# A streaming encoder step on one Trainium2 core: rows of the first norm rounded by ScalarE, scores ahead of the table turns, ten pairs between retrievals, first gates asked for among the up products

## The reference

```
h = rmsnorm(x) ; cb,cc,ch,q,k,v,rg,ga,gb = split(h @ w_in)            # 9 x 1024 columns
conv = causal width-3 convolution of cc*ch, times cb
ret  = chunked retention of rope(q), rope(k), v, 4 heads of 256, with decays and a carried state,
       group norm, times silu(rg)
x += (sigmoid(ga)*conv + sigmoid(gb)*ret) @ w_out
h = rmsnorm(x) ; per token and each of 8 heads: the top 16 of 128x128 product keys
x += sum over picks of softmax(score) * gelu(u[e] . h) * v[e]          # 16384 experts, rows of 1024
y = rmsnorm(x)
```

## Time and profile before

| | |
|---|---|
| median of 3 runs | 2223.83 us (2220.51 to 2227.95) |
| the profiled execution, its own time | 2224.73 us |
| its span, first to last instruction | 2222.9 us (1.8 us of the time lie around it) |
| mean granted TensorE clock | 0.994 |
| PE busy | 2166.9 us, 97% of the span |
| DVE busy | 1730.2 us, 78% |
| POOL busy | 866.3 us, 39% |
| ACT busy | 592.8 us, 27% |
| mean DMA rate | 331 GB/s |

### The profile page before, as it was taken

The page is one execution under the profiler, slowest core; times in us unless marked ns, Lnnn a source line. Parts: engine busy times, 40 slices in busy tenths (PEclk is TensorE's granted clock), DMA queues, the critical chain, the costliest instruction groups (busy, mean ns, idle before and its releaser), DMA issues.

```text
span 2222.9 us, 30818 instructions
## 1 busy us (share of the span) xinstructions
PE 2166.9 (97%) x10473; PEld 1692.8 (76%) x10473; DVE 1730.2 (78%) x3244; ACT 592.8 (27%) x1159; POOL 866.3 (39%) x606
## 2 busy tenths in 40 slices
PE   5999999999999999999999999999999999999998
PEld 5989889899998885655565565577767777777776
DVE  3566675667675285988988989999949898888987
ACT  3212222122223111121221211233324333333333
POOL 4322122223333004576675684512114454454540
PEclk9999999999999999999999999999999999999999
DMA  4999899999983367999999999888899999999993
GB/s 161 304 306 320 288 303 307 318 321 312 309 286 143 108 219 304 355 370 412 403 402 412 389 411 413 337 274 289 292 320 393 413 414 414 413 414 414 414 412 141
DMA packets 314151, 735.40 MB, mean 331 GB/s; under 512 B 30368, under 2 KB 163232, under 8 KB 314016
## 3 DMA queue, kind: packets, MB, share of 16 engines
q1 hardware_dynamic: 189792, 439.67, 54.8%
q0 software_dynamic: 73728, 268.47, 30.6%
q10 hardware_dynamic: 50496, 25.59, 3.8%
HBM read 604.04 MB, written 129.57 MB: 330 GB/s over the span
## 4 chain that ended last, share of the span: by engine, by line
PE 61%; DVE 16%; DMA 7%; issue 6%; POOL 6%; SPq 2%; ACT 1%; DVEq 0%; ACTq 0%; POOLq 0%
PE ps L1750 7%; PE ps L1808 7%; PE ps L1807 7%; PE ps L1809 7%; PE ps L1710 6%; POOL b L679 5%; PE ps L1515 5%; PE ps L1514 5%; DMA b<-in_u_t 5%; PE ps L1516 5%; PE ps L1815 4%; PE ps L1765 3%; DVE b L1392 3%; DMA b<-in_peer_v,b 2%; DVE b L1032 1%
## 5 line engine op out<-in xcount | busy, mean ns | idle before, releaser
L1750 PE MATMUL ps<-b,b 128*128 128x384 f32 x2048 | 665.6, 486 | 0.0
L679 POOL DMA_INDIRECT b<-u_rows,b x256 | 367.2, 1434 | 717.3 <-DVE b L1375 517.9
L1750 PEld LDWEIGHTS ps<-b,b 128*128 128x128 f32 x2048 | 386.8, 190 | 263.4
L644 POOL TENSOR_TENSOR b<-b,b 128x1024 fp32r<-128x1024 f32 x80 | 195.1, 2442 | 468.9 <-ACT b L692 464.4
L1514 PE MATMUL ps<-b,b 128*128 128x320 f32 x1152 | 365.0, 317 | 1.6 <-issue 1.6
L1516 PE MATMUL ps<-b,b 128*128 128x320 f32 x1152 | 357.6, 310 | 0.0
L1515 PE MATMUL ps<-b,b 128*128 128x320 f32 x1152 | 357.5, 310 | 0.0
L1392 DVE SCALAR_TENSOR_TENSOR b<-b,b,b 128x1024 f32<-128x1024 f32 x256 | 330.9, 1292 | 28.3 <-DMA b<-in_peer_v,b 11.2
L1375 DVE CUSTOM_DVE_ANT_0 b<-b,b 128x1024 f32<-128x1024 f32 x256 | 312.5, 1221 | 28.4 <-DMA b<-u_rows,b 22.2
L679 POOL DMA_INDIRECT b<-in_peer_v,b x256 | 291.0, 1137 | 88.6 <-issue 78.3
L1032 DVE STREAM_TRANSPOSE b<-b 128x1024 f32<-128x1024 f32 x128 | 156.9, 1238 | 169.3 <-DMA b<-in_u_t 162.7
(11 more groups left out here) (164 smaller groups left out, 2588.0 us busy)
## 6 DMA issues: line engine op xcount, KB each, us to landing
b<-in_u_t SPq DMA_DIRECT2D x256, 512.0 KB, 5.5
u_rows<-b SPq DMA_DIRECT2D x512, 128.0 KB, 4.3
b<-in_peer_v SPq DMA_DIRECT2D x128, 512.0 KB
b<-in_w_in SPq DMA_DIRECT2D x72, 512.0 KB
b<-in_wq SPq DMA_DIRECT2D x48, 512.0 KB
acts<-b SPq DMA_DIRECT2D x128, 192.0 KB
gates<-b ACTq DMA_DIRECT2D x12, 2048.0 KB
b<-gates SPq DMA_DIRECT2D x32, 768.0 KB
```

Source lines behind the costliest of these rows:

```text
L644: nc.gpsimd.tensor_tensor(lo[u][:, :], raw[:, u, :], hi[u][:, :].bitcast(F32), ALU.subtract).then_inc(lo_ready, 1)
L679: nc.gpsimd.indirect_dma_start(slots[n % SLOTS][:, :], None, u_rows if kind == "u" else v_rows, bass.IndirectOffsetOnAxis(ap=row_id[:, r_ ...
L1750: last = nc.tensor.matmul(ps[:, e % 4, 0:TD], w[:, k * P:(k + 1) * P], h2[:, k, SD:T], start=(k == 0), stop=(k == KT - 1))
```

## The change

It does six things. ACT, not DVE, rounds the rows of the first norm (`rows_high`), and DVE squares and sums the last two of the five tiles. PE's transposes of that norm go to banks 2 to 7 in rotation (`norm_bank`), so that the first product, in banks 0 and 1, no longer waits for the roundings; POOL's `low(A, 0, 0)` moves ahead of all row tiles. In DVE's `scores` the turns stand behind the five multiplications. GAP goes from 11 to 10 and BEFORE_DOWNS from 1 to 6, so three pairs less come before the one-hots and two less among the down products (80 pairs are done when `weigh(0)` is reached, 78 before); all indices for picks, scores and gates move forward by one to three up products. SP reads the first group's activations and gates back within the up products 124 and 126, and the second group behind the first down tile.

```diff
-BEFORE_DOWNS = 1
+BEFORE_DOWNS = 6
+ACTS_AT = 124
+GATES_AT = 126
+SUMS_BY_ACT = 3
-EXP_AT = {1: 7, 2: 36, 3: 64, 4: 93}
-SCORES_AT = {2: 6, 3: 45, 4: 73}
-PICKT_AT = {2: 41, 3: 69, 4: 98}
-GATE_AT = 99
+EXP_AT = {1: 7, 2: 35, 3: 62, 4: 90}
+SCORES_AT = {2: 6, 3: 44, 4: 71}
+PICKT_AT = {2: 40, 3: 67, 4: 95}
+GATE_AT = 96
-GAP = 11
+GAP = 10
-    e = RETRIEVAL_AT + 28.6 * turn + (0.5 + 2.0 * i if i < INSIDE else 17.3 + 0.97 * (i - INSIDE))
+    e = RETRIEVAL_AT + 27.6 * turn + (0.5 + 2.0 * i if i < INSIDE else 17.3 + 0.97 * (i - INSIDE))
...
+def norm_bank(which, tt, b):
+
+    return b if which else 2 + 2 * (tt % 3) + b
...
+            def acts_in(g):
+                for i in range(2):
+                    sp.wait_ge(a_stored[i], 16 * (GROUP // 2) * (g + 1))
+                src = acts[g, :, :, :].rearrange("p k t -> p (k t)")
+                sp.dma_start(al[:, g % 2, :, :].rearrange("p k t -> p (k t)"), src).then_inc(al_loaded[g % 2], 16)
+            def gates_in(g):
+                src = gates[g, :, :, :]
+                sp.dma_start(gr[:, g % 2, :, :, :].rearrange("p b k t -> p b (k t)"), src).then_inc(g_loaded[g % 2], 16)
+            def group_in(g):
+                if g >= 2:
+                    sp.wait_ge(p_ready, (g - 1) * GROUP)
+                gates_in(g)
+                acts_in(g)
...
                 plain_in(3 * A_WQ + e, io["u_t"][e, :, :])
                 if e >= GROUP:
                     acts_out(e - GROUP)
+                if e == ACTS_AT:
+                    sp.wait_ge(onehot_used, TD // 4)
+                    acts_in(0)
+                if e == GATES_AT:
                     for i in range(2):
                         sp.wait_ge(gt_stored[i], 16 * (NB // 2))
+                    gates_in(0)
...
                 down_in(u)
                 acts_out(NKEY - GROUP + u)
                 if u == 0:
-                    group_in(0)
-            group_in(1)
+                    group_in(1)
...
+            low(A, 0, 0)
             for tt in range(TT):
-                if tt == TT - 2:
-                    low(A, 0, 0)
                 rows_low(0, tt, hf)
             for u in range(1, GROUP):
...
-            for tt in range(TT):
+            for tt in range(SUMS_BY_ACT):
                 act.wait_ge(x_loaded[tt], 16)
-                if tt >= 3:
-                    act.wait_ge(sum_done, tt - 2)
-                bank = 2 + 2 * (tt % 3)
+                bank = 2 + 2 * tt
                 nc.scalar.activation(ps[:, bank:bank + 2, :].rearrange("p a b -> p (a b)"), x[:, tt, :], ACT.Square,
                                      accum_out=ss[:, tt:tt + 1]).then_inc(sum_done, 1)
             act.wait_ge(sum_done, TT)
             nc.scalar.activation(rms[:, :], ss[:, :], ACT.Sqrt, bias=eps[:, 0:1], scale=1.0 / D).then_inc(rms_ready, TT)
-            for tt in range(TT):
+            def rows_high(tt):
+                for b in range(2):
+                    act.wait_ge(f_ready, 2 * tt + b + 1)
+                    f = hf[:, b, :].rearrange("p (k t) -> p k t", k=4)
+                    nc.scalar.activation(h_hi[:, 4 * b:4 * b + 4, tt * P:(tt + 1) * P], f, ACT.Copy).then_inc(h_split, 1)
+
+            scale_rows(0, 0, xs)
+            high_a(0, 0, 0, False)
+            for tt in range(1, TT):
                 scale_rows(0, tt, xs)
-                if tt == 1:
-                    high_a(0, 0, 0, False)
+                rows_high(tt - 1)
+            rows_high(TT - 1)
             high_a(1, 1, 1, False)
...
                     f = hf_[:, b, :].rearrange("p (k t) -> p k t", k=4)
-                    hs = (slice(None), slice(4 * b, 4 * b + 4), slice(tt * P, (tt + 1) * P))
-                    line.then(nc.vector.tensor_tensor(f, src, gb, ALU.mult))
-                    nc.vector.tensor_copy(h_hi[hs], f).then_inc(h_split, 1)
-
+                    nc.vector.tensor_tensor(f, src, gb, ALU.mult).then_inc(f_ready, 1)
+
+            for tt in range(SUMS_BY_ACT, TT):
+                dve.wait_ge(x_loaded[tt], 16)
+                squares = yret[:, 2 * (tt - SUMS_BY_ACT):2 * (tt - SUMS_BY_ACT) + 2, :].rearrange("p a b -> p (a b)")
+                nc.vector.tensor_tensor_reduce(squares[:, 0:D], x[:, tt, :], x[:, tt, :], 1.0, 0.0, ALU.mult, ALU.add,
+                                               ss[:, tt:tt + 1]).then_inc(sum_done, 1)
             dve.wait_ge(consts, 16 * 2)
             row_factor(0, 0, TT)
...
             def scores(g, r):
 
                 dve.wait_ge(tabs_loaded, g * 48 + 48)
-                if isinstance(g, int) and g == 0:
-                    turn(16, 2)
                 for j in range(PT + 1):
                     if j == 3:
                         for s in range(PT):
                             then(nc.vector.tensor_scalar(kw[:, s, :], kv[:, s, 0:DK], key_decay(g, s), None, ALU.mult),
                                  kw_ready, g * 12 + (s + 1))
-                        turn(0, 2, r, PER_HEAD)
                     dve.wait_ge(att_done, g * 5 + (j + 1))
                     bank, n = [5, 6, 7, 4, 5][j], att_n[j]
                     then(nc.vector.tensor_tensor(att[:, att_at[j]:att_at[j] + n], ps[:, bank, 0:n],
                                                  dec[:, 0:n] if j < PT else dec_s[:, :], ALU.mult),
                          att_ready, g * 5 + (j + 1))
+                if isinstance(g, int) and g == 0:
+                    turn(16, 2)
                 for s in range(KW - PT):
                     stream_keys(g, s)
                 for i in range(2):
                     then(nc.vector.tensor_tensor(qg[i], qT[:, i, PROMPT:T], gq[:, :], ALU.mult),
                          qg_ready, g * 2 + (i + 1))
+                turn(0, 2, r, PER_HEAD)
...
                     tok = slice(hv * HALF, (hv + 1) * HALF)
                     if rows_from is not None:
 
-                        pe.wait_ge(h_split, rows_from + 2 * TT - 1 + hv)
                         pe.wait_ge(h_ready, rows_from + 2 * -(-(hv + 1) * HALF // P))
...
-                    if tt:
-                        pe.wait_ge(h_ready if which else h_split, which * 2 * TT + 2 * (tt - 1) + b + 1)
+                    if which and tt:
+                        pe.wait_ge(h_ready, which * 2 * TT + 2 * (tt - 1) + b + 1)
+                    if not which and tt >= 3:
+                        pe.wait_ge(f_ready, 2 * (tt - 3) + b + 1)
                     for k in range(4):
                         cols = slice((4 * b + k) * P, (4 * b + k + 1) * P)
-                        last = nc.tensor.transpose(ps[:, b, k * P:(k + 1) * P], xs_[:, tt % 2, cols], ident[:, :])
+                        last = nc.tensor.transpose(ps[:, norm_bank(which, tt, b), k * P:(k + 1) * P], xs_[:, tt % 2, cols],
+                                                   ident[:, :])
```

More of the change, by code:

```diff
@@ L378, in build_program @@
         xsT_done = sem("xsT_done")
+        f_ready = sem("normed_rows_turned")
         h_split = sem("h_split")
@@ L999, in split_rows @@
                     gb = gain[:, 4 * b:4 * b + 4].unsqueeze(2).broadcast_to([P, 4, P])
-                    src = ps[:, b, :].rearrange("p (k t) -> p k t", k=4)
+                    src = ps[:, norm_bank(which, tt, b), :].rearrange("p (k t) -> p k t", k=4)
                     if which == 1:
```

## The result

The changed kernel takes 2230.5 us in the median, the kernel before 2224.4; the ratio is 1.0024, 95% interval 1.0017 to 1.0032. That is slower by a quarter of a per cent, where 2204 was forecast. The profiled execution has a span of 2229.9 us against 2222.9.

The account below looks back on a forecast made before the run. TensorE, busy 2166.9 of 2222.9 us, was taken as the bound, so only its waits and the slow matmuls behind them could shrink. Start 3, mixer 12 and picks 4.5 gave 19.5 us: 2204 by the median, range 2194 to 2214.

Parts of the forecast that it names:

- Gates early, six pairs before the downs: End of the up products: six pairs and the early gates' read stay hidden behind them; 0, from -2 to +1 us.
- That chain is unchanged: Up-to-down transition: ScalarE's way out, its rounding, DVE's two subtractions, first down product stay as before; 0, from -2 to +1.
- The start: First norm: roundings moved to ScalarE bring the first product from 33.26 to 30.3; gain 3 us, from 0 to 5.
- The mixer: Scores ahead of turns, four rounds: old waits go, some for the prompt state's copy appear; gain 12 us, 4 to 21.5.
- rival A: Mixer: waits only move to the prompt state's copy in all four rounds, eating all but 3 us; 2213, chance 0.20.
- Ten pairs: Between retrievals: each pair left out saves DVE 6.5 us, so TensorE's waits for picks go; gain 4.5 us.
- rival C: Between retrievals: pairs cost DVE only its own time, 4.8 us each, so waits for picks grow; 2211, chance 0.10.
- The rival on the other side: Mixer: both moved turns wait their whole loads, prompt state comes 7.4 us later each round; slower, 2244, chance 0.04.

## Why the prediction was wrong

**Gates early, six pairs before the downs** is the step that failed: "Hidden; without that cover each us costs one", taken as 0, from -2 to +1. It cost 17.6 in the trace, 14.8 of it wait and most of the rest the slow matmuls behind it. Three things in it were wrong. First, the store has no price in the step at all. It took at most 13.8 us before, and 44 with more gathers beside it. Second, the cover was counted in TensorE's products, from 119 to 126, seven of 5.16 us. But 126 is a place in SP's list, and SP runs ahead of TensorE: it reached the read at 1631.6, as product 122 ended, 15.7 us after the store was issued. A store of 14 us would just have fitted. "SP may wait there a little" named the place; the wait was 28.3 us. Third, I looked only at DVE for the six pairs ("each needs ScalarE's gelu"), not at POOL and the transfers, though the row with a share of 1.03 was in front of me and used for another step. The section of the Trainium skill that the prediction cites (DMA: Bandwidth & Descriptors, Issuing engines are not separate DMA queues), one set of 16 engines for all, I applied to the pairs and not to the store beside them.

**That chain is unchanged** (from ScalarE's way out at 1667.20 to the first down product 3.3 us later): it held in the changed kernel, 1674.12 to 1677.43. It is only that everything came late in front of it.

**The start:** 3 was forecast, with the first product at 30.3; it began at 28.4, from 33.26, and the lead at the first round was 5.4. The mechanism was right. The half buffers went round in 2.8 us a tile, not 3.1, because the rounding of 512 columns took 0.63 and the handings over were short, and the first difference began at 18.95, not 19.4:

```profile
18.95 2.50 POOL L672 TENSOR_TENSOR b<-b,b 128x512 fp32r<-128x512 f32 x2
...
21.75 2.50 POOL L672 TENSOR_TENSOR b<-b,b 128x512 fp32r<-128x512 f32 x2 [0.30 <-ACT b L760]
...
24.55 2.51 POOL L672 TENSOR_TENSOR b<-b,b 128x512 fp32r<-128x512 f32 x2 [0.29 <-ACT b L760]
```

**The mixer:** 12 was forecast, 2.0 came in this trace, and the runs with and without the new order differ by less than they can tell. The old waits went, as forecast, and were replaced, which is rival A's way. Round 1's new wait and slow matmuls were 5.1 where 4 were forecast, round 4's 6.3 where 4.7 were. The term failed in rounds 2 and 3, forecast at under 1 and with "more room": 2.4 and 3.5. The copy did come earlier in round 2, ending at 235.6 and not at the forecast 238.8; but TensorE wanted it at some 233, and not at 238.0, for the start's gain had not been taken off its time. The terms were added as if each stood alone. And the copy hangs on DVE's own row from `rotate_q` on, 17.5 us without a wait for a tile in round 2; only the run that took the turns out of that row showed this.

**Ten pairs:** 4.5 was forecast and 4.8 came between the first query products and the last up product, where rival C had a loss of 2; in the other traces with ten pairs it is 2.6 to 5.0. What was not in the forecast is that the three pairs left out cost 4 to 5 us among the down products and 1 to 2 in the last norm if nothing takes them up ahead of them. Six ahead did that, at the price above; three do it too.

With these sizes the sum is 5.4 + 2.0 - 1.5 (the `in_wq` waits) + 4.8 - 17.6 = -6.9, which is how late the trace ends. They are stretches of one trace, so they have to add up.

**The rival on the other side** (D, turns without cover, 2244) was slower for another reason than the one that came: the new waits in the mixer never reached 7.3 a round. No rival had a transfer that takes longer because of what the change puts beside it.

Could the 44 us have been seen ahead? An upper estimate from the kernel before was within reach. The store itself holds the engines 7 us. Six pairs gather 24 times 128 rows of 4 KB, 12.6 MB, which is 31 us at the 412 GB/s of the earlier trace rows. If all of it goes first, the store needs 38 us, and more with the tiles, against a cover of 15.7. That it does nearly all go first only the later runs show. How much of the start's gain a given execution keeps varies by a few us between traces of one order, and why stays open.

## What to carry to other kernels

A transfer's duration read from a trace is that of its neighbours then. If an edit brings a burst of large-packet transfers next to a store of many small packets, ask for the time of that store anew, bound it from above, and follow everyone who waits for it: here SP, ScalarE's first rounding and DVE's first weighing. Count the cover of a wait in the list of the engine that waits, not in the list of the one that it feeds. A gain can depend on the other parts, so measure the parts alone and together, and compare the profiled execution's own time with the median first. And moved work wants a place where neither the engine nor the transfers are full: with the read of the gates in the same place, three pairs ahead of the downs were some 12 us faster than six (ratios 0.9963 and 1.0018).

## What the runs showed of the hardware

A 2 MB store in 4112 packets of 512 B took 7.5 to 15.9 us eleven times in the changed kernel, with little or some traffic beside it, then 17.6 beside one pair, 32.9 and 35.8 beside three and four, and 43.9 to 52.9 beside six. In packets of 16 KB it took 11.8 beside six and 12.1 beside four. At 43.9 us that is 48 GB/s, where all transfers together moved 388 in the mean. Its packets held the engines 7 us both at 14 us and at 44. Reads of 768 KB took 4.8 us in runs of 6 KB beside one pair, 15.3 beside six, and 20.1 in runs of 512 B beside four.
